# A Trainium2 kernel of two transformer blocks: large loads first on their queue, small loads held back, modulation rows turned ahead of x, narrow columns multiplied first

## The reference

```python
cos, sin = rope_tables(positions, HEAD_DIM)
mod = jnp.einsum('bd,ldm->lbm', jax.nn.silu(c), w_mod) + b_mod[:, None, :]
sh_m, sc_m, g_m, sh_f, sc_f, g_f = [t[:, None, :] for t in jnp.split(mod[i], 6, axis=-1)]
h = x * (1.0 + sc_m) + sh_m
q_sb, k_sb, v_sb, q_dsa, k_dsa, v_dsa, q_ix, k_ix, w_ix = jnp.split(h @ w_in, idx, axis=-1)
```

## Time and profile before

| what | value |
|---|---|
| median of 3 runs | 1142.61 us (1140.88 to 1143.27) |
| the profiled execution | 1144.01 us, with a span of 1142.7 us |
| TensorE busy | 1124.9 us (98% of the span) |
| VectorE busy | 842.5 us (74%) |
| ScalarE busy | 627.6 us (55%) |
| GpSimd busy | 81.1 us (7%) |
| moved by DMA | 232.22 MB, 203 GB/s in the mean |
| mean granted TensorE clock | 0.998 |

### The profile page before, as it was taken

The page is one execution under the profiler, slowest core; times in us unless marked ns, Lnnn a source line. Parts: engine busy times, 40 slices in busy tenths (PEclk is TensorE's granted clock), DMA queues, the critical chain, the costliest instruction groups (busy, mean ns, idle before and its releaser), DMA issues.

```text
span 1142.7 us, 24990 instructions
## 1 busy us (share of the span) xinstructions
PE 1124.9 (98%) x10534; PEld 1079.2 (94%) x10534; DVE 842.5 (74%) x1429; ACT 627.6 (55%) x1075; POOL 81.1 (7%) x103
## 2 busy tenths in 40 slices
PE   8999999999999999999999999999999999999998
PEld 6998799999998999999999999999999999999987
DVE  5698879988876888897575589578565677676643
ACT  3467556645435588666444455734645566555542
POOL 3000013000012000111000034100000000000000
PEclk9999999999999999999999999999999999999999
DMA  9977755899997643566655642843345463655540
GB/s 322 381 235 275 245 176 180 301 327 306 313 313 242 202 148 116 182 217 219 219 185 166 212 149 75 259 149 113 109 150 185 148 221 102 213 189 183 197 170 37
DMA packets 194687, 232.22 MB, mean 203 GB/s; under 512 B 4083, under 2 KB 169555, under 8 KB 194576
## 3 DMA queue, kind: packets, MB, share of 16 engines
q1 hardware_dynamic: 193984, 230.32, 60.6%
q0 software_dynamic: 592, 0.31, 0.2%
HBM read 229.56 MB, written 1.05 MB: 202 GB/s over the span
## 4 chain that ended last, share of the span: by engine, by line
PE 91%; DVE 4%; DMA 2%; issue 1%; ACT 1%; POOL 0%; SPq 0%; DVEq 0%
PE ps L154 90%; PE ps L157 2%; DMA XR<-in_x_dram 1%; DVE hL L196 1%; DVE wlo L187 1%; DMA raw<-in_w_in_even_dram 1%; DVE T L187 1%; DMA MW<-in_w_mod_dram 0%; DVE LT L187 0%; DVE T L196 0%; POOL T L187 0%; DVE XA L193 0%; DVE MR L196 0%; DVE ST L199 0%; ACT RD L166 0%
## 5 line engine op out<-in xcount | busy, mean ns | idle before, releaser
L187 DVE TENSOR_TENSOR wlo<-raw,whi 128x1024 fp32r<-128x1024 f32 (+1 forms) x346 | 409.9, 1206 | 162.3 <-ACT whi L166 161.0
L154 PE MATMUL ps<-hH,whi 128*128 128x256 f32 (+3 forms) x1792 | 517.2, 289 | 2.2 <-DVE hL L196 1.9
L154 PE MATMUL ps<-hH,wlo 128*128 128x256 f32 (+3 forms) x1792 | 504.6, 282 | 1.1 <-DVE wlo L187 1.1
L154 PE MATMUL ps<-hL,whi 128*128 128x256 f32 (+3 forms) x1792 | 505.0, 282 | 0.0
L166 ACT ACTIVATE whi<-raw 128x1024 fp32r<-128x1024 f32 (+1 forms) x346 | 349.5, 1033 | 193.3 <-PE ps L154 131.7
L154 PEld LDWEIGHTS ps<-hH,whi 128*128 128x128 f32 x1792 | 337.8, 189 | 8.8 <-issue 4.5
L154 PEld LDWEIGHTS ps<-hH,wlo 128*128 128x128 f32 x1792 | 338.1, 189 | 1.3 <-DVE wlo L187 1.3
L154 PEld LDWEIGHTS ps<-hL,whi 128*128 128x128 f32 x1792 | 338.4, 189 | 0.4
L154 PE MATMUL ps<-uL,whi 128*128 128x256 f32 x352 | 99.2, 282 | 0.0
L154 PE MATMUL ps<-uH,whi 128*128 128x256 f32 x352 | 99.0, 281 | 0.0
L154 PE MATMUL ps<-uH,wlo 128*128 128x256 f32 x352 | 98.4, 280 | 0.0
(11 more groups left out here) (314 smaller groups left out, 1614.4 us busy)
## 6 DMA issues: line engine op xcount, KB each, us to landing
MW<-in_w_mod_dram SPq DMA_DIRECT2D x47, 1024.0 KB, 6.9
raw<-in_w_up_dram SPq DMA_DIRECT2D x44, 1024.0 KB, 5.5
raw<-in_w_in_dram SPq DMA_DIRECT2D x36, 1024.0 KB, 5.0
raw<-in_w_down_dram SPq DMA_DIRECT2D x27, 1024.0 KB, 6.2
raw<-in_w_gate_dram SPq DMA_DIRECT2D x22, 1024.0 KB, 7.3
raw<-in_w_in_odd_dram SPq DMA_DIRECT2D x12, 1024.0 KB, 7.3
raw<-in_w_in_even_dram SPq DMA_DIRECT2D x8, 1024.0 KB, 9.6
raw<-in_w_down_dram SPq DMA_DIRECT2D x8, 768.0 KB, 6.7
```

The costliest lines, as they stand in the source:

```text
L154: return self.queued(self.e.matmul(out, lhsT, rhs, start=start, stop=stop, skip_group_check=True, **kw), length if pos is None else max(le ...
L187: return self.queued(self.e.tensor_tensor(out, a, b, op), 0.07 + cols(out) / self.RATE)
```

## The change

It does six things in `begin`, `even`, `plan_weights` and `vectors`:

- The loads of c, of the identity and of the modulation bias go to ScalarE's own queue; SyncE's queue begins with the first modulation weight.
- GpSimd's load of the positions waits until the fourth modulation weight has landed (`mod_loaded[3]`), its other 17 loads until the sixth has (`mod_loaded[5]`).
- The rope angles are no longer computed in the opening but in a track, `rope_tables`, that starts when the positions are loaded.
- TensorE turns the rows of modulation 0 and 1 before it turns x, and `modulated` of the first two blocks is placed behind the first of the four copies of the turned x.
- Step 0 multiplies the narrow columns of both blocks, then the wide columns of both, and the raw halves are used in this order.
- One dummy product stands before the first product of h, for four.

```diff
--- before.py
+++ after.py
@@ -276,7 +276,7 @@
     p.even_first = []
     for s in range(4):
         p.even_first.append((p.slot(W, 2048, 452, 2 * s, 2), p.slot(W, 0, 1024, 2 * s, 2)))
-        if s < 3:
+        if 0 < s < 3:
             p.together(*p.even_first[s])
         else:
             p.whole(*p.even_first[s])
@@ -694,19 +694,16 @@
     pe, act, dve, pool, sp, m, D_ = k.pe, k.act, k.dve, k.pool, k.sp, k.m, k.D
     RV = m.RV
     vec = lambda a: a.rearrange("l (r p) -> (l r) p", p=128)
-    pos_in = pool.dma(m.PI, D_["positions"].to_broadcast([128, S]), k.into["pos"])
-    k.meta_in = pool.dma(m.MTR, D_["meta_tokens_2"], k.into["meta"])
+    k.rows_in = k.meta_in = k.rope_tables = None
     rows_ = [(2, 16 * i, vec(D_[n])) for i, n in enumerate(("ln_mix_g", "ln_mix_b", "ln_ffn_g", "ln_ffn_b"))]
     rows_ += [(2, 64, D_["subln_g"]), (2, 65, D_["hgrn_norm_w_2"])]
     rows_ += [(3, 0, vec(D_["lb_param_2"])), (3, 16, vec(D_["attn_norm_w_2"])),
               (3, 24, D_["conv_w_2"].rearrange("o l (r p) -> (o l r) p", p=128)), (3, 48, vec(D_["ffn_norm_w_2"]))]
     rows_ += [(4, 0, D_["ffn_conv_w_2"].rearrange("o l (r p) -> (o l r) p", p=128)), (4, 66, vec(D_["ffn_conv_b_2"]))]
     rows_ += [(5, i, D_[n]) for i, n in enumerate(("lam_q1", "lam_k1", "lam_q2", "lam_k2"))]
-    for g, r, src in rows_:
-        k.rows_in = pool.dma(RV[r:r + src.shape[0], g, 0:src.shape[1]], src, k.into["rows"])
-    c_in = sp.dma(RV[0:8, 0, :], vec(D_["c"]), k.into["c"])
-    ident_in = sp.dma(m.CST[:, 0:K_TRI], D_["cst"][:, 0:K_TRI], k.into["ident"])
-    bm_in = sp.dma(RV[0:96, 1, :], vec(D_["b_mod"]), k.into["bm"])
+    c_in = k.act_dma.dma(RV[0:8, 0, :], vec(D_["c"]), k.into["c"])
+    ident_in = k.act_dma.dma(m.CST[:, 0:K_TRI], D_["cst"][:, 0:K_TRI], k.into["ident"])
+    bm_in = k.act_dma.dma(RV[0:96, 1, :], vec(D_["b_mod"]), k.into["bm"])
     k.first_loads = list("mmxwwmmwwmmwwmmww")
     load_first(k)
     x_in = sp.dma(m.XR, D_["x"].rearrange("b (t p) d -> p (b t) d", p=128), k.into["x"])
@@ -743,25 +740,47 @@
             dve.ts(v, v, 1.0, ALU.add)
     k.b_mod = dve.inc()
 
-    ang, turns, r = m.ANG
-    inv, sgn = m.CST[:, K_INV:K_INV + 1], m.CST[:, K_SGN:K_SGN + 1]
-    dve.wait_ge(*pos_in).wait_ge(*ident_in).copy(ang, m.PI).settle().ts(ang, ang, inv, ALU.mult)
-    for out, turn_ in ((m.SIN, 0.0), (m.COS, 0.25)):
-        dve.settle().ts(turns, ang, 1.0 / TWO_PI, ALU.mult, turn_, ALU.add)
-        dve.settle().ts(turns, turns, MAGIC, ALU.add).settle().ts(turns, turns, -MAGIC, ALU.add)
-        dve.settle()
-        if out is m.COS:
-            dve.wait_ge(*sine)
-        dve.stt(r, turns, -C1, ang, ALU.mult, ALU.add)
-        dve.settle().stt(r, turns, -C2, r, ALU.mult, ALU.add).settle().stt(r, turns, -C3, r, ALU.mult, ALU.add)
-        dve.settle().ts(r, r, turn_ * TWO_PI, ALU.add, 3.1415925, ALU.min)
-        angle = dve.settle().ts(r, r, -3.1415925, ALU.max).inc()
-
-        sine = act.wait_ge(*angle).act(out, r, ACT.Sin, scale=sgn if out is m.SIN else 1.0).inc()
-    k.rope_tables = sine
+    def late_loads():
+        while 3 not in k.mod_loaded:
+            yield None
+        yield due(k.mod_loaded[3])
+        pos_in = pool.wait_ge(*k.mod_loaded[3]).dma(m.PI, D_["positions"].to_broadcast([128, S]), k.into["pos"])
+        start(k, rope_tables(pos_in))
+        while 5 not in k.mod_loaded:
+            yield None
+        yield due(k.mod_loaded[5])
+        k.meta_in = pool.wait_ge(*k.mod_loaded[5]).dma(m.MTR, D_["meta_tokens_2"], k.into["meta"])
+        for g, r, src in rows_:
+            rows_in = pool.dma(RV[r:r + src.shape[0], g, 0:src.shape[1]], src, k.into["rows"])
+        k.rows_in = rows_in
+
+    def rope_tables(pos_in):
+        ang, turns, r = m.ANG
+        inv, sgn = m.CST[:, K_INV:K_INV + 1], m.CST[:, K_SGN:K_SGN + 1]
+        sine = None
+        yield due(pos_in)
+        dve.wait_ge(*pos_in).wait_ge(*ident_in).copy(ang, m.PI).settle().ts(ang, ang, inv, ALU.mult)
+        for out, turn_ in ((m.SIN, 0.0), (m.COS, 0.25)):
+            yield dve.clock
+            dve.settle().ts(turns, ang, 1.0 / TWO_PI, ALU.mult, turn_, ALU.add)
+            dve.settle().ts(turns, turns, MAGIC, ALU.add).settle().ts(turns, turns, -MAGIC, ALU.add)
+            yield dve.clock
+            dve.settle()
+            if sine:
+                dve.wait_ge(*sine)
+            dve.stt(r, turns, -C1, ang, ALU.mult, ALU.add)
+            yield dve.clock
+            dve.settle().stt(r, turns, -C2, r, ALU.mult, ALU.add).settle().stt(r, turns, -C3, r, ALU.mult, ALU.add)
+            yield dve.clock
+            dve.settle().ts(r, r, turn_ * TWO_PI, ALU.add, 3.1415925, ALU.min)
+            angle = dve.settle().ts(r, r, -3.1415925, ALU.max).inc()
+            yield due(angle)
+            sine = act.wait_ge(*angle).act(out, r, ACT.Sin, scale=sgn if out is m.SIN else 1.0).inc()
+        k.rope_tables = sine
 
 
     pace(k, lambda: due(x_in))
+    pace(k, lambda: 0.0 if MODS[1] in k.mod else None)
     pe.wait_ge(*x_in)
     k.x_cols = [None] * KD
 
@@ -772,14 +791,20 @@
                 pe.tr(m.ps[b][:, at:at + 128], m.XR[:, t, (2 * j2 + i) * 128:(2 * j2 + i + 1) * 128], ident)
         return pe.inc()
 
-    for j2 in range(4):
-        b = (4, 5, 6, 4)[j2]
-        if j2 < 2:
-            pe.wait_ge(*(silu, bm)[j2])
-        elif j2 == 3:
-            fill(k, b)
+    def x_columns(j2, b):
         turned = transpose(j2, b)
         k.x_cols[2 * j2] = k.x_cols[2 * j2 + 1] = act.wait_ge(*turned).act(m.LT[:, 512 * j2:512 * j2 + 512], m.ps[b], ACT.Copy).inc(k.bank[b])
+        return turned
+
+    pe.wait_ge(*silu)
+    x_columns(0, 4)
+    modulated(k, 0)
+    modulated(k, 1)
+    pe.wait_ge(*bm)
+    x_columns(1, 5)
+    x_columns(2, 6)
+    fill(k, 4)
+    turned = x_columns(3, 4)
     turn(k)
 
     def centred():
@@ -803,6 +828,7 @@
             k.x[2 * j2] = k.x[2 * j2 + 1] = act.wait_ge(*columns_).act(X, pair(m.ps[b]), ACT.Copy, scale=ALPHA).inc(k.bank[b])
 
     k.q = {}
+    start(k, late_loads())
     start(k, centred())
 
     def masks():
@@ -819,6 +845,8 @@
     ident = m.CST[:, K_ID:K_ID + 128]
     b0, b1 = 4 + 2 * lane, 5 + 2 * lane
     p0, p1 = m.ps[b0], m.ps[b1]
+    while k.rows_in is None:
+        yield None
     yield due(k.rows_in, k.meta_in)
     yield from emptied(k, b0, b1)
     fill(k, b0, b1)
@@ -1045,24 +1073,29 @@
     k.rope_jobs, k.roped = [], {}
     banks = (0, 1, 2, 4, 5, 6)
     widths = (128, 128, 128, 68) + (128,) * 8
-    fill_next(k, *banks)
     y = [None] * 6
     for s in range(4):
-        modulated(k, 2 * s)
-        modulated(k, 2 * s + 1)
-        if s == 0:
-            keep_clock(k, 4)
+        if s > 0:
+            modulated(k, 2 * s)
+            modulated(k, 2 * s + 1)
         jobs = []
         for i, w in enumerate(widths):
             bank, n, wide = banks[i // 2], i % 2, i >= 4
             at = 128 * (i - 4 * wide)
             jobs.append((m.ps[bank][0:w, n * S:n * S + S], P.even_first[s][wide], slice(at, at + w), n == 0))
-        if s < 3:
-            multiply(k, jobs, (0, 1), h, 2 * s, TOK, k.h_low, s == 0, False, True)
+        if s == 0:
+            fill_next(k, 0, 1)
+            keep_clock(k, 1)
+            multiply(k, jobs[:4], (0, 1), h, 0, TOK, k.h_low, True, False, True)
+            fill_next(k, *banks[2:])
+            multiply(k, jobs[4:], (0, 1), h, 0, TOK, k.h_low, True, False)
+        elif s < 3:
+            multiply(k, jobs, (0, 1), h, 2 * s, TOK, k.h_low, False, False, True)
         else:
             y[0] = y[1] = multiply(k, jobs[:4], (0, 1), h, 2 * s, TOK, k.h_low, False, True, True)
             start(k, keys(k, y[:2]))
             y[2:] = [multiply(k, jobs[4:], (0, 1), h, 2 * s, TOK, k.h_low, False, True)] * 4
+    pace(k, lambda: due(k.rope_tables) if k.rope_tables else None)
     k.mods_soon = 8
     k.act.table(SET_EXP)
     k.k_, k.v, k.scored, k.chosen = {}, {}, None, None
@@ -2413,6 +2446,7 @@
         sem = lambda name: ctx.enter_context(nc.semaphore(name))
         k.pe, k.act, k.dve = Tensor(nc.tensor, sem("pe_done")), Scalar(nc.scalar, sem("act_done")), Vector(nc.vector, sem("dve_done"))
         k.pool, k.sp = Loader(nc.gpsimd, sem("pool_done")), Loader(nc.sync, None)
+        k.act_dma = Loader(nc.scalar, None)
         k.raw_in = [Counter(sem(f"raw{i}_in")) for i in range(RAW)]
         k.mod_in = [Counter(sem(f"mod{i}_in")) for i in range(6)]
         k.into = {n: Counter(sem(n + "_in")) for n in ("c", "ident", "cst", "bm", "x", "rows", "pos", "meta", "fnw")}
```

## The result

The change makes the kernel slower. The median is 1151.98 us (4 runs, 1151.26 to 1153.65) against 1142.33 us, ratio 1.009 with a 95% interval of [1.0077, 1.0102]: 9.65 us more where I forecast 1.5 less. The profiled execution took 1151.26 us, with a span of 1150.0. The one before had a span of 1142.7, so the two traces are 7.3 us apart, and some 2.4 of the 9.65 us cannot be looked for in them.

What follows compares the result with a forecast made beforehand. The prediction took TensorE's dense run from 21.68 us, and the chain from x landing before it, as the bound; a 2.7 us lead less 1.2 us at the third step gave -1.5 from 1142.61, so 1141.1 us, range 1138.9 to 1144.0.

Steps and rivals of the forecast that it cites:

- The lead of 2.7 us: Opening loads: x lands 2.7 us earlier, 1.33 from earlier issue on SyncE and 1.37 from holding back GpSimd's loads.
- rival D: Opening loads: the first load lands no earlier than its 1.33 us, giving 1142.5 us; chance 0.06.
- my own sign (before 12.2): Opening: x landing later than 14 us or before 12.2 us would show the forecast wrong.
- From x to the dense run: Opening, first turn of x to first wlo product: 6.07 us against 6.13 before, a gain of 0.06 us.
- Three of the dummy products are gone, which were beside a wait.: Opening, before the first product of h: one dummy product for four, given no cost in the forecast.
- rival A: TensorE idle before the first whi or at the third step: clock halves once, 1.5 us lost, 1142.6 us; chance 0.28.
- The third step: Moved rope work makes hL late: TensorE waits 1.6 us, and the third step starts 1.2 us later by the old clock.
- the order of small work: First fifth of TensorE's instructions: order changes a little, allowed 0.7 us to either side; beyond that, order unchanged.
- The cover: From 24 to 45 us: weights in place ahead of use hide the held back loads at no cost; uncovered, up to 1.97 us.
- Rival C: VectorE bounds the third and fourth steps: TensorE waits at both, the clock falls behind each, 1145.7 us; chance 0.07.

Runs made afterwards that it cites:

- e1_small_sp: The changed kernel with the loads of c, identity and bias back at the head of SyncE's queue; 1149.92 us.
- e5_whi: The changed kernel with the first whi on ScalarE placed ahead of the last three copies of the turned x; 1149.64 us.
- e11_free: The changed kernel, all work done, but the planner charged nothing for the rope operations when it sets the order; 1154.99 us.
- e16_b_open: The kernel before with modulation rows ahead of x, hH and hL behind the first copy, narrow columns first and eight dummies meant to run during the copies; 1145.30 us.
- e12_b_mods: The kernel before with modulation rows 0 and 1 turned before x, and hH and hL of two blocks behind the first copy; 1146.05 us.
- e10_thin: The changed kernel with VectorE's rope operations cut from 256 columns to 8, the planner still charged full length; 1149.93 us.

## Why the prediction was wrong

- **The lead of 2.7 us.** The issue (0.74 us) and the bytes (2.4 us' worth more in the first 10 us) came as forecast, and x landed 4.2 us earlier, at 11.3 us: rival D is out, and by my own sign (before 12.2) the size of this part was wrong too. The step that failed is the one from x landing to x turned: "They go to ScalarE's queue, which is otherwise only loading a table then. So all large loads, x among them, are issued 1.33 us earlier: that much is certain." It is true of the issue, but it priced the three small loads by what they take from the large ones, and not by when they themselves land. They are the head of TensorE's chain: c, bias, 8 dummies, two modulation products and now their turned rows, all ahead of x. Measured: x turned 0.16 us later, not 2.7 earlier; the queue costs 2.06 us in the changed kernel and 2.3 in the kernel before (with the tables early it costs nothing that shows). The rule that I quoted from the Trainium skill, DMA: Bandwidth & Descriptors, section "Issuing engines are not separate DMA queues" (issuing from another engine saves only issue time), agrees with the rows: x was issued 1.3 us earlier than in e1_small_sp and landed 1.3 us earlier. It speaks of the gain alone, and I took it for the whole effect. The other 2.9 us of x's earlier landing came with GpSimd's loads, for which I had taken 1.37.
- **From x to the dense run.** 6.00 us for 6.07, whi behind three copies as read: right, and confirmed from the other side by e5_whi.
- **"Three of the dummy products are gone, which were beside a wait."** Wrong: behind the 3.06 us wait the clock fell. This was rival A, at 1.5 us; at 30 us the dummies are worth 2.6 us, at the end 1.3.
- **The third step.** The wait for hL is 1.79 us for 1.6, at the place worked out. The length is right; both its ends lie some 5 us later than forecast, TensorE ready at 47.4 us for 42.2. But the sum ended there. The second step that failed is "up to there the order of small work changes a little, for which I allow 0.7 us to either side". The moved tables cost 8.38 us with the order that they bring, and only 2.05 of them are the time of the rope work; one order of eight loads is worth 2.20.
- **The cover.** "so they cost nothing", of the held loads, was right only in that no TensorE wait for a DMA of weights shows. With 17 of the 18 held back, and nothing else changed, the kernel before is 3.4 us slower in the median.
- **The range.** 1151.98 lies 8 us above it. Rival C, at 0.07, was the nearest in kind (two late waits with a slow clock behind) and 6.3 us too low. Its second wait, at the fourth step, did not come, the one for QS did, and behind the first the clock stayed up.

## What to carry to other kernels

When a small load moves to another queue, ask first who waits for it, and follow that engine's queue to the next large load that matters; only then count what the large loads gain. A load that lands earlier is worth something only if the engine that takes it is ready. When the order comes from a planner with estimated clocks, moving one block of work is a change of the whole order behind it. How many rows move is a warning (181 here, 38 in the version that lost little), but no price: 161 moved in e11_free, which loses 12.6 us, 158 in e16_b_open, which loses 2.4, and 21 in e12_b_mods, which loses 3.6. And a lead at the start counts only once nothing behind takes it back: leads of 2.6 us at 30 us were 1.3 to 2.1 us at the end here.

## What was unexpected of the hardware

The identity's 81 KB took 4.6 us to land when issued at 1.38 us on a second queue beside megabyte loads, and 2.0 us near the head of SyncE's queue. One load of 128 KB by GpSimd made x land some 2 to 2.7 us later. And the clock is not told by the length of a wait alone. In the changed kernel the wait of 1.79 us at 49.21 us was followed by a granted clock of 1.00. Behind 1.84 us at 46.63 in e1_small_sp it was 0.50:

```profile
48.00:49.00 1.00, 1.00 (x24) 0.92 (x24) 0.02 (x1) 1.00 (x2) 0.00 (x0) 0.50 0.99 401
```

Behind the wait of 1.57 us for QS it was 0.50 at 75 us in the changed kernel and 1.00 in e10_thin and e5_whi. Whether this also changes from one execution of a kernel to the next is not shown, since each has one trace.
